# Forgetting attention: q and k staged whole and placed by transfers, value products in two passes, outputs split per head pair

## The reference, cut to what matters

```python
proj = x @ w_in
q, k, v, f_logit = jnp.split(proj, [D, 2 * D, 3 * D], axis=-1)
log_f = jax.nn.log_sigmoid((f_logit + b_f).astype(F32))
c = jnp.cumsum(log_f, axis=1).transpose(0, 2, 1)
s = jnp.einsum('bhqd,bhkd->bhqk', qb, k, preferred_element_type=F32) * scale
s = s + cb[..., None] - c[:, :, None, :]
s = jnp.where(pb[:, None] >= k_pos[None, :], s, -jnp.inf)
p = jax.nn.softmax(s, axis=-1)
o = jnp.einsum('bhqk,bhkd->bhqd', p.astype(v.dtype), v)   # then o @ w_o
```

## Time and profile before

| what | value |
|---|---|
| median of three executions | 1889.77 us (1886.86 to 1890.77) |
| the profiled execution, its own time | 1891.8 us |
| its span (first to last instruction) | 1890.0 us |
| granted TensorE clock, share of full | 0.996 |
| PE busy | 1864.4 us (99%) |
| DVE busy | 927.0 us (49%) |
| ACT busy | 718.7 us (38%) |

### The profile page before, as it was taken

How to read it: one execution, slowest core, us unless ns; L and a number is a source line. 1 busy time by engine, 2 the same in 40 slices (tenths; PEclk the granted TensorE clock), 3 DMA queues, 4 the chain that set the end, 5 groups by cost and what they waited for, 6 DMA issues and landing times.

```text
span 1890.0 us, 24133 instructions
## 1 busy us (share of the span) xinstructions
PE 1864.4 (99%) x8779; PEld 1534.4 (81%) x8779; DVE 927.0 (49%) x1336; ACT 718.7 (38%) x1177; POOL 24.5 (1%) x44
## 2 busy tenths in 40 slices
PE   9999999999998999999999999999999999999998
PEld 6888888877776888888888888888887788888888
DVE  5444434356886544444334444433478644444332
ACT  4223223246775423222333322323378432322332
POOL 1000000000000000000000000000000000000000
PEclk9999999999999999999999999999998999999999
DMA  4222223321111222222333222223311122222332
GB/s 158 99 100 94 92 87 105 121 97 65 52 56 41 99 95 100 90 98 86 102 112 105 95 100 94 89 96 105 117 56 57 68 100 89 99 100 84 97 102 86
DMA packets 55881, 174.36 MB, mean 92 GB/s; under 512 B 6672, under 2 KB 9232, under 8 KB 55824
## 3 DMA queue, kind: packets, MB, share of 16 engines
q1 hardware_dynamic: 55680, 173.57, 27.0%
q10 hardware_dynamic: 144, 0.03, 0.0%
HBM read 171.48 MB, written 2.10 MB: 92 GB/s over the span
## 4 chain that ended last, share of the span: by engine, by line
PE 95%; ACT 2%; DVE 1%; issue 1%; DMA 0%; POOL 0%; SPq 0%; DVEq 0%; POOLq 0%; ACTq 0%
PE bank L432 90%; PE bank L778 1%; PE bank L790 1%; ACT scratch L1322 1%; PE bank L888 0%; ACT wide_hi L1278 0%; ACT wide_hi L1270 0%; DMA scratch<-x_dram 0%; PE bank L458 0%; PE bank L492 0%; ACT w_hi L993 0%; PE bank L495 0%; PE bank L501 0%; DVE w_lo L1396 0%; PE bank L902 0%
## 5 line engine op out<-in xcount | busy, mean ns | idle before, releaser
L1396 DVE TENSOR_TENSOR w_lo<-raw,w_hi 128x1024 fp32r<-128x1024 f32 (+1 forms) x343 | 392.4, 1144 | 821.1 <-ACT w_hi L993 819.9
L993 ACT ACTIVATE w_hi<-raw 128x1024 fp32r<-128x1024 f32 (+1 forms) x343 | 341.3, 995 | 846.4 <-PE bank L432 843.9
L432 PE MATMUL bank<-u_hi,w_hi 128*128 128x512 f32 (+1 forms) x1592 | 630.7, 396 | 0.3 <-DVE w_lo L1396 0.3
L432 PE MATMUL bank<-u_hi,w_lo 128*128 128x512 f32 (+1 forms) x1592 | 620.7, 390 | 0.0
L432 PE MATMUL bank<-u_lo,w_hi 128*128 128x512 f32 (+1 forms) x1592 | 620.5, 390 | 0.0
L432 PEld LDWEIGHTS bank<-u_hi,w_lo 128*128 128x128 f32 (+1 forms) x1592 | 298.4, 187 | 63.8
L432 PEld LDWEIGHTS bank<-u_hi,w_hi 128*128 128x128 f32 (+1 forms) x1592 | 298.7, 188 | 61.1 <-issue 1.1
L432 PEld LDWEIGHTS bank<-u_lo,w_hi 128*128 128x128 f32 (+1 forms) x1592 | 298.7, 188 | 59.4 <-issue 1.0
L432 PE MATMUL bank<-wide_hi,w_hi 128*128 128x512 f32 (+1 forms) x816 | 317.0, 388 | 0.7 <-issue 0.4
L432 PE MATMUL bank<-wide_lo,w_hi 128*128 128x512 f32 (+1 forms) x816 | 315.3, 386 | 0.0
L432 PE MATMUL bank<-wide_hi,w_lo 128*128 128x512 f32 (+1 forms) x816 | 315.1, 386 | 0.0
(11 more groups left out here) (186 smaller groups left out, 1292.3 us busy)
## 6 DMA issues: line engine op xcount, KB each, us to landing
raw<-ffn_in_dram SPq DMA_DIRECT2D x175, 512.0 KB, 3.2
raw<-ffn_out_dram SPq DMA_DIRECT2D x128, 384.0 KB, 2.9
raw<-mix_w_dram SPq DMA_DIRECT2D x51, 512.0 KB, 3.2
y_dram<-raw SPq DMA_DIRECT2D x8, 256.0 KB, 2.7
scratch<-x_dram SPq DMA_DIRECT2D x2, 512.0 KB, 8.7
raw<-ffn_in_dram SPq DMA_DIRECT2D x2, 256.0 KB, 3.5
scratch<-x_dram SPq DMA_DIRECT2D x2, 256.0 KB, 4.7
sq<-x_dram SPq DMA_DIRECT2D x1, 512.0 KB, 10.6
```

The costliest lines, as they stand in the source:

```text
L432: mm = pe.matmul(out, a, b, start=first and k == 0, stop=last and k == n - 1)
L993: act.activation(w_hi[:, slot, 0:cols], raw[:, (base + r) % RAW, 0:cols], ACT.Copy)\
L1396: dve.tensor_tensor(w_lo[:, s, 0:cols], raw[:, r, 0:cols], f32(w_hi[:, s, 0:cols]), ALU.subtract).then_inc(w_ready, 1)
```

## The change

Four things change, all in the forgetting attention.

- **V side by side.** ACT writes the high part of V and DVE the low part so that each head has 64 columns of high part and then 64 of low (`v_heads`). A value block is two passes: [V high | V low] x P high gives 128 rows of bank 7, and V high x P low adds into the upper 64 rows.
- **Sum of the halves.** After value 3 ACT copies rows 64 to 127 of bank 7 to `diag` (64x512), and DVE adds them to rows 0 to 63 into `sq` (64x512, `o_summed`, which frees bank 7).
- **Outputs per pair.** Every second step (t odd from 3, and t = 16) ACT makes the high part of a pair from `sq` (128x512) and DVE the low part (128x512, `o_ready`, now one a pair).
- **q and k.** For all pairs but the first, ACT writes one high part (128x512) and DVE one low part (128x512) to a staging place, and SP issues six SBUF-to-SBUF transfers of 64x512 (128 KB each), four of the high part and two of the low part, to the places that the scores read. The scores of a pair's first head wait for all of them (`qk_moved`). DVE's low part now comes ahead of those of turns 2 and 3.

```diff
+            def place_qk(t):
+
+                j, is_q = t // 2 + 1, t % 2 == 0
+                stage = slice(FOX_STAGE_AT, FOX_STAGE_AT + SEQ)
+                sp.wait_ge(qk_hi_ready, t + 3)
+                sp.wait_ge(scored, TB * (t + 1))
+                for par in range(2):
+                    own = slice(64 * par, 64 * par + 64)
+                    at = FOX_Q_AT[par][j % 2] if is_q else FOX_K_AT[par]
+                    for to in (wide_hi[own, at:at + SEQ],
+                               wide_hi[beside(par), at:at + SEQ] if is_q else wide_lo[own, at:at + SEQ]):
+                        sp.dma_start(f32(to), f32(wide_hi[own, stage])).then_inc(qk_moved, 16)
+                sp.wait_ge(qk_ready, t + 3)
+                for par in range(2):
+                    own = slice(64 * par, 64 * par + 64)
+                    at = FOX_Q_AT[par][j % 2] if is_q else FOX_K_AT[par]
+                    to = wide_lo[own, at:at + SEQ] if is_q else wide_hi[beside(par), at:at + SEQ]
+                    sp.dma_start(f32(to), f32(wide_lo[own, stage])).then_inc(qk_moved, 16)
+
...
                     at = TB * t + kb
                     pe.wait_ge(pt_ready, at + 1)
                     if kb == 0:
-                        pe.wait_ge(*((o_ready, t) if t else (v_ready, 2 * TB)))
-                    v_at = V_AT + kb * D + t * DH
+                        pe.wait_ge(*((o_summed, t) if t else (v_ready, 2 * TB)))
+                    v = v_heads(kb, t, 1)[:, 0, :, :]
                     p_at = PT_AT + (at % 2) * SEQ
                     cols = SEQ - kb * P
-                    products(bank[7][0:DH, kb * P:SEQ],
-                             [(wide(v_at, v_at + DH), wide(p_at, p_at + cols))], kb == 0, kb == TB - 1)\
-                        .then_inc(pv_done, 1)
+                    out = bank[7][:, kb * P:SEQ]
+                    if kb == 0:
+                        pe.matmul(out, v, wide_hi[:, p_at:p_at + cols], start=True, stop=False)
+                    mm = pe.matmul(out[0:DH, :], v[:, 0, :], wide_lo[:, p_at:p_at + cols], start=False, stop=False)
+                    if kb > 0:
+                        mm = pe.matmul(out, v, wide_hi[:, p_at:p_at + cols], start=False, stop=kb == TB - 1)
+                    mm.then_inc(pv_done, 1)
 
...
                                 pe.wait_ge(picked, t + 1)
-                                pe.wait_ge(qk_copied, 2 * j + 2)
-                                pe.wait_ge(qk_ready, 2 * j + 2)
+                                if j == 0:
+                                    pe.wait_ge(qk_copied, 2)
+                                    pe.wait_ge(qk_ready, 2)
+                                else:
+                                    pe.wait_ge(qk_moved, 96 * 2 * j)
...
+            def output_hi(m):
+
+                act.wait_ge(o_summed, 2 * m + 2)
+                act.activation(wide_hi[:, O_AT + m * SEQ:O_AT + (m + 1) * SEQ], sq[:, m % 2, :], ACT.Copy)\
+                   .then_inc(o_hi_ready, 1)
+
+            def project_hi(t):
+
+                act.wait_ge(qk_scaled, t + 3)
+                if t:
+                    act.wait_ge(qk_moved, 96 * t)
+                act.activation(wide_hi[:, FOX_STAGE_AT:FOX_STAGE_AT + SEQ], scaled[:, :], ACT.Copy)\
+                   .then_inc(qk_hi_ready, 1)
...
+                def output_lo(m):
+
+                    a = O_AT + m * SEQ
+                    dve.wait_ge(o_hi_ready, m + 1)
+                    dve.tensor_tensor(wide_lo[:, a:a + SEQ], sq[:, m % 2, :], f32(wide_hi[:, a:a + SEQ]), ALU.subtract)\
+                       .then_inc(o_ready, 1)
+
+                def project_lo(t):
+                    stage = slice(FOX_STAGE_AT, FOX_STAGE_AT + SEQ)
+                    dve.wait_ge(qk_hi_ready, t + 3)
+                    dve.tensor_tensor(wide_lo[:, stage], scaled[:, :], f32(wide_hi[:, stage]), ALU.subtract)\
+                       .then_inc(qk_ready, 1)
...
+                    if t >= 3 and t % 2:
+                        output_hi((t - 3) // 2)
                     if t:
-                        par, jo = (t - 1) % 2, (t - 1) // 2
                         act.wait_ge(pv_done, TB * t)
-                        act.activation(wide_hi[64 * par:64 * par + 64, O_AT + jo * SEQ:O_AT + (jo + 1) * SEQ],
-                                       bank[7][0:DH, :], ACT.Copy).then_inc(o_hi_ready, 1)
+                        if t >= 2:
+                            act.wait_ge(o_summed, t - 1)
+                        act.activation(diag[0:DH, :], bank[7][DH:2 * DH, :], ACT.Copy).then_inc(o_lower, 1)
+                    if t == HEADS:
+                        output_hi(PAIRS - 1)
...
+                        dve.wait_ge(o_lower, t)
+                        if t % 2 and t >= 5:
+                            dve.wait_ge(o_ready, (t - 3) // 2)
+                        dve.tensor_tensor(sq[64 * ((t - 1) % 2):64 * ((t - 1) % 2) + 64, (t - 1) // 2 % 2, :],
+                                          bank[7][0:DH, :], diag[0:DH, :], ALU.add).then_inc(o_summed, 1)
+                        if t >= 3 and t % 2:
+                            output_lo((t - 3) // 2)
+                        if t == HEADS:
+                            output_lo(PAIRS - 1)
```

More of the change, by code:

```diff
@@ L197, in build @@
         pv_done = sem("pv_done")
+        o_lower = sem("o_lower")
+        o_summed = sem("o_summed")
         o_hi_ready = sem("o_hi_ready")
@@ L272, in build, with v_heads @@
         VS_AT = V_AT + SEQ
+        def v_heads(t, first, count):
+            part = (wide_hi, wide_lo)[t // 2]
+            a = V_AT + t % 2 * 2 * D + first * 2 * DH
+            return part[:, a:a + count * 2 * DH].rearrange("p (h s c) -> p h s c", s=2, c=DH)
         block = ctx.enter_context(nc.Block())
@@ L341, in load_mixer, with load_fox @@
                     load((base + n) % RAW, mix_w[first + n], UNIT, base + n - RAW + 1)
+            def place_qk(t):
[15 more added lines that the diff above has]
+                    sp.dma_start(f32(to), f32(wide_lo[own, stage])).then_inc(qk_moved, 16)
+            def load_fox():
+                for u in range(FOX_UNITS):
+                    t = u - 17
+                    if 0 <= t < 2 * PAIRS - 2:
+                        place_qk(t)
+                    load((FOX_BASE + u) % RAW, mix_w[u], UNIT, FOX_BASE + u - RAW + 1)
             load_ffn(0)
-            load_mixer(FOX_BASE, 0, FOX_UNITS)
+            load_fox()
             load_ffn(1)
@@ L812, in fillers @@
                         yield from project(n + m - 2, m % 2, (qk_scaled, m - 1))
-                    yield from first_out_pairs(n + 2 * PAIRS - 2, [0] * 7 + [1], (qk_scaled, 2 * PAIRS), o_ready, 2,
+                    yield from first_out_pairs(n + 2 * PAIRS - 2, [0] * 7 + [1], (qk_scaled, 2 * PAIRS), o_ready, 1,
                                                (expd, TB * HEADS))
@@ L859, in fox @@
                             value(t - 1, s[1])
-                mixer_out_stage(n - len(WO_KBS), nn + 1, fill, o_ready, 2)
+                mixer_out_stage(n - len(WO_KBS), nn + 1, fill, o_ready, 1)
             def window(nn):
@@ L1195, in fox @@
                             act.wait_ge(rstd_ready, nn + 1)
-                            a = V_AT + t * D + (k // 4) * 512
-                            act.activation(wide_hi[:, a:a + 512], bank[4 * (k // 4) + t][:, :], ACT.Copy,
+                            act.activation(v_heads(t, 8 * (k // 4), 8)[:, :, 0, :],
+                                           bank[4 * (k // 4) + t].rearrange("p (h c) -> p h c", c=DH), ACT.Copy,
                                            scale=rstd[:, t:t + 1]).then_inc(v_hi_ready, 1)
@@ L1624, in project_scaled @@
                         dve.wait_ge(qk_ready, count)
-                        dve.wait_ge(qk_copied, count)
+                        dve.wait_ge(qk_copied, min(count, 2))
                     dve.wait_ge(unit_used, n + 1)
@@ L1718, in fox @@
                     if t:
-                        par, jo = (t - 1) % 2, (t - 1) // 2
-                        rows = slice(64 * par, 64 * par + 64)
-                        a = O_AT + jo * SEQ
-                        dve.wait_ge(o_hi_ready, t)
-                        dve.tensor_tensor(wide_lo[rows, a:a + SEQ], bank[7][0:DH, :], f32(wide_hi[rows, a:a + SEQ]),
-                                          ALU.subtract).then_inc(o_ready, 1)
+                        dve.wait_ge(o_lower, t)
[7 more added lines that the diff above has]
+                            output_lo(PAIRS - 1)
                     if j + 1 < PAIRS or t == HEADS - 1:
```

41 lines of the change are left out of this document (21 added, 20 removed).

## The result

The changed kernel takes 1910.11 us (1904.73 to 1912.65, 4 runs) against 1888.82 us (4 runs) for the kernel before, run on the same chip: a ratio of 1.011, 95% interval 1.0094 to 1.0126, slower by 21 us. The forecast was 1895.0, with a range of 1887 to 1902.5: the direction was right, the size was not. The profiled execution has a span of 1906.9 us, 16.9 above the one of before.

What follows compares the result with a forecast made beforehand. PE was taken to bound the kernel, busy throughout attention steps 1 to 12. Passes -8.7, k's transfers +10.5 and the end +3.4 us sum to +5.2, forecasting 1895.0 us, range 1887 to 1902.5.

Steps and rivals of the forecast that it cites:

- The passes: Value product on PE: one pass of each block goes, 0.59 us a head, 9.4 us; gain 8.7 after the wide-weight charge.
- The charge for the wide weights: Last value block of each head: loading 128-column weights costs 0.045 us more, 0.7 us over 16 heads.
- rival 4: Wide weights cost PE a load in every value block, 2.9 us instead of 0.7: 1897.2 us; chance 0.05.
- ACT and DVE: Inside an attention step both engines get lighter, but PE waited for neither, so nothing was counted.
- rival 2: k's transfers are hidden or faster, scores never wait, only the end costs: 1884.5 us; chance 0.12.
- The transfers of k: Ahead of a pair's first scores: last landing after 4.55 us with 3.05 available, wait 1.5 us, seven times, 10.5 us.
- rival 3: k's transfers move one after the other at half rate, 0.6 us each: 1902.4 us; chance 0.16.
- The end: End of the attention: losses of 2.0 us at step 16 and 1.4 us at the last pair's output, together 3.4 us.

Runs made afterwards that it cites:

- the sorted version: Changed kernel with k's transfers sorted by head, one filler ahead of score 3 in even steps 2 to 12, outputs of pair 6 made in step 14: 1881.5 us.
- The value part alone: Kernel before plus two-pass value products and outputs per pair, q and k still written by ACT and DVE, no transfers: 1895.5 us.
- two queues: Changed kernel with two of the four high-part transfers issued by ACT's queue, so SP issues four instead of six: 1907.4 us.
- half the columns: Changed kernel with its six transfers cut to 256 of 512 columns (64 KB each), scores partly from stale columns: 1907.0 us.
- the transfers' part alone: Kernel before plus q and k staged and placed by transfers, value products in three passes and outputs per head as before: 1911.9 us.
- fillers first: Changed kernel with two filling products moved ahead of score 3 in even steps 2 to 12: 1896.3 us.

## Why the prediction was wrong

**The passes: right, and sized a little low.** In the sorted version two steps fall by 1.18 us, 0.59 a head where 0.54 were forecast. The charge for the wide weights was right where it was laid: the last pass of a head took 0.06 us to the next start before,

```profile
517.57 0.22 PE L432 MATMUL bank<-wide_hi,wide_lo 128*64 128x128 f32 x1
517.63 0.46 PE L432 MATMUL bank<-u_hi,w_hi 128*128 128x512 f32 x1
```

and takes 0.11 with weights of 128 columns in the changed kernel:

```profile
499.17 0.28 PE L845 MATMUL bank<-wide_hi,wide_lo 128*128 128x128 f32 x1
499.28 0.45 PE L469 MATMUL bank<-u_hi,w_hi 128*128 128x512 f32 x1
```

The longer blocks gain all that a pass costs, so rival 4 is out.

**ACT and DVE: right for the changed kernel, for the wrong reason.** "PE did not wait for either, so I count nothing" took the busy PE of before as proof that both engines were early enough. They were for a step of 10.2 us. The value part alone shows that with the old work on q and k they are late for a shorter one: the lighter work is what the gain of the passes stands on. Rival 2 is right that it needs hidden transfers, and the sorted version came out at 1881.5 where rival 2 had 1884.5, with 2.2 us of the end's loss taken back.

**The transfers of k: the term that was sized too small.** The wait was put at 1.5 us and was 2.37. The 3.05 us available (3.16 measured: 497.71 to 500.87) and the landing of 2.3 were right; the failed term is the spacing, taken as 0.45 from the stores where it is 0.64 (0.50 once): the sixth issue began 3.07 us after the first instead of 2.25, 0.82 later, and the wait was 0.87 longer. The stores move 256 KB of full rows to memory, and no row showed that their spacing holds for these transfers. So the wait term was 10.5 us and measured 16.6, with about 1.6 more for the restarts. Rival 3, with a chance of 0.16, had a wait of 2.55 from half the rate; the runs show that limit and beside it the queue's, either of which alone gives about the measured wait, so that rival 3 came near for half of the reason. The Trainium skill (SBUF — State Buffer, section "Door 1: The DMA port swizzle") has about 218 GB/s for 64 partitions, and by an estimate worked out from it 128 KB take 0.60 us. The trace comes near where the queue is not the limit: 232 GB/s over six of them. So the Trainium skill bore on this case more than the nearest rows did. That a queue issued these transfers no faster than one in about 0.6 us was in no row and in no term of the prediction.

**The clock: the step that failed outright, put at nothing without a reason.** "PE waits 1.5 us" was priced as idle time alone. Before, the clock was 1.00 all through the attention; whether it would stay there behind a new wait was not asked. It cost 7.9 us, and without them the measured 1910.1 would be 1902.2, just inside the range. That rival 3's 1902.4 and 7.9 make 1910.3 is partly luck, since its terms differ from the measured ones.

**The end: right, with some luck.** 3.4 forecast, waits of 2.2 and 1.4 us, at the two places named. But a wait of 2.2 us can cost the clock here too: nine versions have it at the start of step 16, and in seven of them a stretch at the lower clock stands at it or behind it. The changed kernel's profiled execution is one of the two without.

## What to carry to other kernels

A wait of some 2 us that is put on a busy TensorE can cost more than its length: ask what the clock does behind it. Waits that were cut to 1 us or less cost their length and little more here. Cost a chain of small SBUF-to-SBUF transfers by the number of issues in a queue and by the partitions they cover, and send first what is waited for first. A bound engine at 100%, with its neighbours at 75 to 85%, does not mean that they are early enough for a shorter step: follow their order and work out when each operand is ready at the new pace.

## What the runs showed of the hardware

- SP issues these transfers 0.64 us apart, whether they move 64 or 128 KB on 64 partitions, and takes 0.55 to 0.61 us for each of 256 KB on 128; the weight loads' issues take 0.33 us. Landing takes 2.0 us for 64 KB, 2.3 for 128, 2.5 for 256 KB on 128 partitions.
- Six transfers of 128 KB on 64 partitions, in two queues, move 232 GB/s with the DMA engines at 0.90; three of 256 KB on 128 partitions, in one queue, 357 GB/s at 0.96.
- TensorE's clock fell to the lower level behind 5 of 7 waits of 2.37 us in the changed kernel, 5 of 7 of 2.1 with two queues, 5 of 7 of 2.0 with half the columns, 7 of 7 of 1.8 to 2.9 in the transfers' part alone, and behind the one of 2.33 with fillers first. Behind the waits for transfers of 0.4 to 1.3 us, 26 in four versions, no fall followed before the next waits. Near the attention's end it fell behind the wait of 2.2 us at step 16 in 7 of 9 versions, and in four behind two waits close together, of 0.7 and 0.9 us or 0.6 and 1.3. Each fall behind a wait of 2.37 us cost about 1.6 us. Why it falls behind some waits and not behind others of the same length is open.
- With a float32 pass of 128 columns, weights of 128 columns in place of 64 raised its cost from 0.06 to 0.11 us; with passes of 256 columns or more nothing shows.
